# Crossing the rotary rows with small transfers in place of TensorE's sparse products, in a two-block fp32 layer stack on one core

## The chip, the cores and the metric

One NeuronCore of one Trainium2 chip runs the whole program in one launch. The metric is the device time of that launch in microseconds (us), the median of three runs. Engines are written as in the profile: PE is TensorE, DVE is VectorE, ACT is ScalarE, POOL is GpSimd, SP is SyncE, which only issues transfers. "ACTq" and "SPq" are rows of an engine's instruction sequencer (here the issuing of a transfer).

## The reference, cut to what matters

Two blocks run one behind the other on x of shape 1 x 256 x 1024 in fp32. The first is two layers of feed-forward, mixer, feed-forward. The second puts 16 meta tokens in front (L = 272 tokens) and runs two "hybrid" layers, each a sliding-window attention beside an mLSTM. The change is in the rotary step of that attention:

```python
q = rms_norm_2(aq.reshape(B, L, ATT_HEADS, ATT_HEAD_DIM), q_norm_g)
k = rms_norm_2(ak.reshape(B, L, ATT_KV_HEADS, ATT_HEAD_DIM), k_norm_g)
q = apply_partial_rope(q, cos, sin)
k = apply_partial_rope(k, cos, sin)

def apply_partial_rope(x, cos, sin):
    half = ROT_DIM // 2                       # 8
    x1, x2, rest = x[..., :half], x[..., half:ROT_DIM], x[..., ROT_DIM:]
    out = concatenate([x1 * c - x2 * s, x2 * c + x1 * s, rest])
```

Heads have 64 elements, of which the first 16 are rotated: element d (0 to 7) is mixed with element d + 8. There are 16 query heads and 2 key heads.

## The kernel before, in words

Activations lie transposed: 128 features on the partitions, tokens along the row. A 128-row chunk holds two heads. In each hybrid layer the keys are chunk c = 0 and the queries are chunks c = 1 to 8. Everything is fp32; a weight tile is split by ACT into a rounded part (`w_hi`, L1127) and by DVE into the rest (`w_lo`, L1865; every fifth unit has both in `y_both`), and PE multiplies three products for each tile (L690).

Weights come in "units" of 512 KB (up to four 128-row slabs of 256 columns) in a ring of four raw buffers, five for the split parts. The split of a unit is issued three to four units ahead of its use, between the other work of ACT and DVE, in the order of the program text. A hybrid layer streams its units in the order of `STREAM`: kv (units 0 and 1), mif (2, 3), aq (4 to 11), mqk (12 to 19), then mv, mo, ag, mg. What else is done beside unit u is in the table `VISITS`: for the rotary, `("turn", c)` at unit 5 for c = 0 and at 6 + 2 * ((c - 1) // 2) for c = 1 to 8, and `("turned", c)` at unit 5 and at 8 + 2 * ((c - 1) // 2). After it come `rt` (units 14, 15), `kx` (16) and the attention itself (`att`, from unit 18).

For one chunk, before the change:

- ACT copies the projected tile from PSUM to `k_att` or `q` (`raw_tile`, L1452), and squares it for the norm (`turn`, L1463).
- POOL multiplies it by the sine table into `qs` (L1827) and by the gained cosine table `cos_g` into `qc` (L1828). From the third chunk on it first waits for DVE's add of the chunk two before, because `qs` and `qc` have two buffers.
- PE multiplies `qs` by the 128 x 128 matrix `rot_g` (L933), which has a few +-gain entries and is otherwise zero, into PSUM.
- DVE adds that product to `qc` (`turn`, L2315) and so writes the rotated chunk back.

`tables` (L2260 to L2263) makes `cos_g` and `rot_g` on DVE once a layer. ACT's work in unit 1 of a layer is the copy of the key tile (L1452); in layer 0 the two square roots of the closing norm of the first block follow straight behind it (table load L1159, L1622, L1625), and DVE's reciprocal of L1622's result (L1887) makes `rstd`, by which every projected tile is scaled.

At the start of the program SP issues four weight loads (L540), the meta tokens (L589) and 17 small parameter loads (`parameters`, L529 and L533), and only then goes on with the weights.

## Time and profile before

| | us |
|---|---|
| median of 3 runs (lowest, highest) | 1448.73 (1448.48, 1448.89) |
| the profiled execution | 1448.88 |
| its span, first to last instruction | 1447.1 |
| PE busy | 1430.4 (99%) |
| DVE busy | 1094.8 (76%) |
| ACT busy | 854.0 (59%) |
| POOL busy | 273.1 (19%) |
| mean granted TensorE clock | 0.999 |

The chain that ended last is by engine PE 81%, DVE 11%, ACT 4%, issue 2%, DMA 1%. The transfer engines' queue of SP has 53.8% of their time, that of ACT 0.8%. The busy share is a mean over stages: PE at 99% does not say that every stage waits for PE, since a matmul's record begins when it may run and neighbours overlap; which engine is late in a stretch is read from the chain and from the idle times with their releasers. The program's stretches are: the first block up to about 915 us, hybrid layer 0 up to about 1182 us, hybrid layer 1 from there on.

### The profile page before, as it was taken

What the parts mean: (1) busy time and instruction counts of PE and PEld (TensorE: products, weight loads), DVE (VectorE), ACT (ScalarE), POOL (GpSimd) and SP (SyncE); (2) the same over time, 40 slices, a digit from 0 to 9 for tenths busy, and PEclk for the clock granted to TensorE, in tenths of its full rate; (3) what the DMA queues carried; (4) which work ended last, traced back from release to release, by engine and by line L of the source; (5) the groups of instructions that cost most, each with busy time, mean ns of one, the idle gap of its engine ahead of it and who ended that gap; (6) DMA issues with size and microseconds to landing.
All of it is one profiled execution on the core that took longest, in us unless ns stands there. A gap on an engine that the chain in (4) does not pass through costs nothing.

```text
span 1447.1 us, 27305 instructions
## 1 busy us (share of the span) xinstructions
PE 1430.4 (99%) x9633; PEld 1318.5 (91%) x9633; DVE 1094.8 (76%) x2031; ACT 854.0 (59%) x1559; POOL 273.1 (19%) x329
## 2 busy tenths in 40 slices
PE   8999999999999999999999999999999999999998
PEld 7888899988888888889988888999999999999998
DVE  6777679877756777667787766898878779976883
ACT  6665458766544666446566554656757555576762
POOL 1111113121102111014031113332250035121000
PEclk9999999999999999999999999999999999999999
DMA  6667754566565666565556565544344555434533
GB/s 211 197 194 211 233 180 131 179 185 202 183 188 182 192 187 197 185 197 164 159 171 200 181 188 175 165 143 125 89 127 142 164 154 154 127 101 123 147 119 118
DMA packets 247875, 241.25 MB, mean 167 GB/s; under 512 B 15456, under 2 KB 246736, under 8 KB 247784
## 3 DMA queue, kind: packets, MB, share of 16 engines
q1 hardware_dynamic: 244888, 236.73, 53.8%
q10 hardware_dynamic: 2896, 3.30, 0.8%
q8 instruction: 58, 0.95, 0.3%
q14 instruction: 33, 0.27, 0.1%
HBM read 238.92 MB, written 1.07 MB: 166 GB/s over the span
## 4 chain that ended last, share of the span: by engine, by line
PE 81%; DVE 11%; ACT 4%; issue 2%; DMA 1%; ACTq 0%; SPq 0%; DVEq 0%
PE bank L690 74%; DVE w_lo L1865 3%; ACT w_hi L1127 1%; DVE work L2467 1%; DVE work L2416 1%; PE bank L1010 1%; DVE work L1902 1%; PE bank L994 1%; DMA raw<-in_w_out_dram 1%; DVE y_both L1865 1%; DMA raw<-in_ffn_w_in_dram 1%; DVE work L2490 1%; PE bank L977 1%; PE bank L923 1%; ACT L1159 0%
## 5 line engine op out<-in xcount | busy, mean ns | idle before, releaser
L690 PE MATMUL bank<-x_both,w_hi 128*128 128x512 f32 (+2 forms) x3216 | 747.8, 336 | 0.9 <-DVE w_lo L1865 0.5
L1865 DVE TENSOR_TENSOR w_lo<-raw,w_hi 128x1024 fp32r<-128x1024 f32 (+1 forms) x429 | 519.4, 1234 | 203.8 <-ACT w_hi L1127 202.8
L1127 ACT CAST w_hi<-raw 128x1024 fp32r<-128x1024 f32 (+1 forms) x429 | 429.3, 1028 | 126.5 <-PE bank L690 108.2
L690 PEld LDWEIGHTS bank<-x_both,w_hi 128*128 128x128 f32 x3216 | 467.8, 189 | 3.9 <-DVE w_lo L1865 1.3
L690 PEld LDWEIGHTS bank<-x_both,w_lo 128*128 128x128 f32 x2312 | 405.8, 188 | 62.5
L690 PE MATMUL bank<-x_both,w_lo 128*128 128x256 f32 (+1 forms) x2312 | 462.2, 281 | 0.0
L690 PE MATMUL bank<-y_both,w_hi 128*128 128x512 f32 (+2 forms) x1376 | 331.5, 342 | 1.8 <-DVE w_lo L1865 1.0
L690 PEld LDWEIGHTS bank<-y_both,w_lo 128*128 128x128 f32 x1040 | 184.3, 188 | 31.3
L690 PE MATMUL bank<-y_both,w_lo 128*128 128x256 f32 (+1 forms) x1040 | 206.1, 280 | 0.0
L690 PEld LDWEIGHTS bank<-y_both,w_hi 128*128 128x128 f32 x1376 | 200.3, 189 | 2.8 <-DVE w_lo L1865 1.4
L1752 POOL TENSOR_TENSOR work<-work,rstd 128x256 f32<-128x256 f32 x88 | 67.0, 783 | 412.0 <-ACT work L1196 412.0
L1178 ACT COPY pre<-bank 128x256 f32<-128x256 f32 x176 | 56.9, 375 | 67.2 <-PE bank L690 66.9
L1208 ACT CAST y_both<-work 128x256 f32 (+1 forms) x88 | 32.7, 406 | 59.5 <-DVE work L1933 59.4
L690 PE MATMUL bank<-x_both,y_both 128*128 128x272 f32 (+1 forms) x504 | 67.6, 289 | 0.0
L1196 ACT ACTIVATE work<-work 128x256 f32<-128x256 f32 x88 | 33.2, 418 | 53.2 <-DVE work L1922 53.2
L690 PEld LDWEIGHTS bank<-x_both,y_both 128*128 128x128 f32 x504 | 63.6, 188 | 0.6
L1138 ACT ACTIVATE x_both<-h,par 128x256 fp32r<-128x256 f32 (+1 forms) x56 | 28.1, 512 | 60.6 <-DVE h L1978 52.9
L1813 POOL TENSOR_SCALAR work<-work 128x256 f32<-128x256 f32 x32 | 36.4, 1137 | 98.0 <-DVE work L2390 98.0
L1717 POOL TENSOR_TENSOR sq<-h 128x256 f32<-128x256 f32 (+1 forms) x34 | 21.4, 631 | 163.2 <-DVE h L1978 162.9
L1882 DVE SCALAR_TENSOR_TENSOR x_both<-h,par,x_both 128x256 fp32r<-128x256 f32 (+1 forms) x56 | 29.1, 528 | 25.6 <-ACT x_both L1138 25.6
L1940 DVE TENSOR_TENSOR y_both<-work,y_both 128x256 f32 (+1 forms) x88 | 33.6, 423 | 15.3 <-ACT y_both L1208 14.7
L1902 DVE TENSOR_TENSOR work<-bank,rstd 128x256 f32<-128x256 f32 (+1 forms) x98 | 37.4, 422 | 5.2 <-PE bank L690 4.9
(312 smaller groups left out, 1394.9 us busy)
## 6 DMA issues: line engine op xcount, KB each, us to landing
raw<-in_ffn_w_in_dram SPq DMA_DIRECT2D x176, 512.0 KB, 4.2
raw<-in_w_in_dram SPq DMA_DIRECT2D x100, 512.0 KB, 3.6
raw<-in_ffn_w_out_dram SPq DMA_DIRECT2D x64, 512.0 KB, 4.5
raw<-in_w_out_dram SPq DMA_DIRECT2D x32, 512.0 KB, 4.2
raw<-in_ffn_w_out_dram SPq DMA_DIRECT2D x32, 384.0 KB, 3.6
raw<-in_rec_w_in_dram SPq DMA_DIRECT2D x16, 512.0 KB, 4.0
raw<-in_sg_w_in_dram SPq DMA_DIRECT2D x16, 512.0 KB, 4.3
raw<-in_rec_w_out_dram SPq DMA_DIRECT2D x8, 512.0 KB, 3.5
```

The costliest lines, as they stand in the source:

```text
L690: i_ = mm(accs[m][:, cols], w[:, j, m * P:(m + 1) * P], moving, start=begin and g == 0 and not residual, stop=final)
L1127: nc.scalar.copy(hi_part(U)[:, 0:n, :], raw[:, s, 0:n, :]).then_inc(hi_made, 1)
L1138: i_ = activation(xview(dst, k, N), src, ACT.Copy, scale=scale)
L1178: nc.scalar.copy(ffn_b[:, m, :], bank[b][:, SEQ:2 * SEQ]).then_inc(low_copied, 1)
L1196: activation(ffn_s[:, m, :], ffn_t[:, m, :], ACT.Silu).then_inc(silu_done, 1)
L1208: nc.scalar.copy(dst, ffn_h[:, m, :]).then_inc(act_hi, 1)
L1752: TT(ffn_r[:, m, :], ffn_s[:, m, :], rstd[:, META:L], MUL).then_inc(gate_scaled, 1)
L1813: TS(pr[:, P:AW], pr[:, P:AW], rec[:, 1:2], None, MUL).then_inc(s_prob, 1)
L1865: TT(lo_part(U)[:, 0:n, :], raw[:, s, 0:n, :], hi_part(U)[:, 0:n, :].bitcast(fp32), SUB).then_inc(lo_made, 1)
L1882: i_ = STT(out=xview(dst_lo, k, N), in0=src, scalar=scale, in1=hi, op0=MUL, op1=SUB)
L1902: TT(dst, tile(pr, m, N), rstd[:, T0:L], MUL).then_inc(tile_read, 1)
L1940: TT(lo, ffn_h[:, m, :], hi.bitcast(fp32), SUB).then_inc(act_ready, 1)
```

## The change: rows crossed by transfers

- The matrix `rot`, the tile `rot_g` and PE's products are removed; PE's `turned` does nothing.
- New in ACT: `cross` issues four transfers from on-chip memory to on-chip memory. Each takes eight rows of the tile and puts them on the eight rows they are rotated with (0 to 7 with 8 to 15, and the same at 64). One call serves the key tile (8 rows x 272 each), one call each pair of query chunks (8 rows x 2 x 272, or 2 x 256 in layer 1): five calls and 20 transfers a layer. A call first waits for its copies.
- `crossed_k` is the last chunk of `qk`, `crossed_q` is `mv`; both are free at that time.
- POOL waits for the transfers and multiplies the crossed rows by `sin_g`, the sine table with its sign and the crossed gain in it. DVE makes `sin_g` where it made `rot_g`.
- DVE adds `qs` and `qc`, both from on-chip memory, and waits for POOL instead of PE.
- SP issues six more small parameter loads (the gains with their eights exchanged) in `parameters`.

```diff
-        rot_g = region(2, P)
+        sin_g = region(2)
+        crossed_k, crossed_q = qk[:, NC8 - 1, :], mv
+        crossed = [sem(f"crossed{i}") for i in range(5)]
...
+                half = ROT // 2
+                for n, src in (("attn_q_crossed", attn_q_norm_g_2), ("attn_k_crossed", attn_k_norm_g_2)):
+                    t, r, k = PAR[n]
+                    both = par_rows[r:r + k, t, :].rearrange("l (e d) -> l e d", e=2)
+                    for a, b, w in ((0, half, half), (half, 0, half), (ROT, ROT, DH - ROT)):
+                        g = src[:, b:b + w].rearrange("l (o d) -> l o d", o=1).broadcast_to((k, 2, w))
+                        sp.dma_start(both[:, :, a:a + w], g).then_inc(par_loaded, 16)
...
-                pe.wait_ge(par_loaded, 16 * 17)
+                pe.wait_ge(par_loaded, 16 * 23)
...
-                def turned(c):
...
-                    mm(bank[5 + n % 2][:, 0:L], rot_g[:, 0 if c else 1, :], qs[:, n % 2, :], start=True,
-                       stop=True).then_inc(rot_mm, 1)
...
+                def cross(i, src, dst, landed):
+
+                    half = ROT // 2
+                    act.wait_ge(tile_read, landed)
+                    for a in (0, DH):
+                        for x, y in ((a, a + half), (a + half, a)):
+                            act.dma_start(dst[x:x + half], src[y:y + half]).then_inc(crossed[i], 16)
...
                                 raw_tile(pb, 0, k_att, L)
+                                cross(4, k_att, crossed_k, 2 * pb + 1)
...
                                         raw_tile(pb + p, m, q[:, 2 * p + m, T0:L], L - T0)
+                                    cross(p, q[:, 2 * p:2 * p + 2, T0:L], crossed_q[:, 2 * p:2 * p + 2, T0:L], T + 2)
...
-                    TT(qs[:, n % 2, :], src, cst("sin"), MUL)
+                    pool.wait_ge(crossed[(c - 1) // 2 if c else 4], 64 * (l + 1))
+                    TT(qs[:, n % 2, :], crossed_q[:, c - 1, :] if c else crossed_k, sin_g[:, 0 if c else 1, :], MUL)
...
-                    TS(rot_g[:, 0, :], cst("rot"), gq, sc, MUL, MUL)
-                    TS(rot_g[:, 1, :], cst("rot"), gk, None, MUL).then_inc(cos_ready, 1)
+                    TS(sin_g[:, 0, :], cst("sin"), pcol("attn_q_crossed", l), sc, MUL, MUL)
+                    TS(sin_g[:, 1, :], cst("sin"), pcol("attn_k_crossed", l), None, MUL).then_inc(cos_ready, 1)
...
-                    dve.wait_ge(rot_mm, n + 1)
-                    TT(dst, bank[5 + n % 2][:, 0:L], qc[:, n % 2, :], ADD).then_inc(q_ready, 1)
+                    dve.wait_ge(qc_new, n + 1)
+                    TT(dst, qs[:, n % 2, :], qc[:, n % 2, :], ADD).then_inc(q_ready, 1)
```

ACT's instructions in unit 1 of layer 0, before (L1452 is the copy of the key tile, L1159 and L1622 the root and its table; names in brackets are the semaphores waited for):

```order
L1127 CAST y_both<-raw 128x1024 [waits unit_done,w_loaded0]
L1452 COPY work<-bank 128x272 [waits first_done,tile_read]
L1159 ACT_TABLE_LOAD
L1159 ACTIVATE root_of_eps<-epsc 128x1
L1622 ACTIVATE rms<-bank,eps_sq 128x272 [waits sum_done]
```

and in the changed kernel, whose line numbers differ by a few:

```order
L1122 CAST y_both<-raw 128x1024 [waits unit_done,w_loaded0]
L1447 COPY work<-bank 128x272 [waits first_done,tile_read]
L1455 DMA work<-work 8x272 [waits tile_read]
L1455 DMA work<-work 8x272 x3
L1154 ACT_TABLE_LOAD
L1154 ACTIVATE root_of_eps<-epsc 128x1
L1626 ACTIVATE rms<-bank,eps_sq 128x272 [waits sum_done]
```

Four transfers now stand between the key tile's copy and the root, with a wait for that copy. In the aq units the same four (8x544) stand between the two copies and the squares.

SP's parameter loads at the program's start, before:

```order
L529 DMA par_rows<-in_rec_gate_x_b_dram 8x128
L533 DMA par_rows<-in_attn_q_norm_g_dram 2x64 x2
L533 DMA par_rows<-in_attn_k_norm_g_dram 2x64 x2
L591 UNCONDITIONAL_BRANCH
L591 ISA
L540 ISA [waits lo_made]
L540 DMA raw<-in_ffn_w_in_dram 128x4x256
```

and in the changed kernel:

```order
L527 DMA par_rows<-in_rec_gate_x_b_dram 8x128
L531 DMA par_rows<-in_attn_q_norm_g_dram 2x64 x2
L531 DMA par_rows<-in_attn_k_norm_g_dram 2x64 x2
L538 DMA par_rows<-in_attn_q_norm_g_dram 2x2x8 x2
L538 DMA par_rows<-in_attn_q_norm_g_dram 2x2x48
L538 DMA par_rows<-in_attn_k_norm_g_dram 2x2x8 x2
L538 DMA par_rows<-in_attn_k_norm_g_dram 2x2x48
L596 UNCONDITIONAL_BRANCH
L596 ISA
L545 ISA [waits lo_made]
L545 DMA raw<-in_ffn_w_in_dram 128x4x256
```

Six loads now stand in front of the fifth weight load.

## Rows read from the trace of the kernel before

**Rows 1.** Busy time by engine in one stretch: us, busy us of each engine.

```profile
927.10:946.40 19.30, 19.30 (x158) 19.07 (x157) 18.91 (x22) 10.96 (x19) 9.73 (x8) 1.00 0.64 184
```

**Rows 2.** The chain that ended last, 915 to 1000 us: start, length, what.

```profile
939.35 1.02 PE bank L933 x4
...
946.48 1.05 ACT w_hi L1127
947.53 1.21 DVE y_both L1865
...
996.09 0.47 DVE work L2362 x2
...
996.60 0.49 PE bank L993 x2
```

**Rows 3.** Line L933, whole run: count, ns min/median/max, first and last start.

```profile
L933 PE MATMUL bank<-work x36: 392/393/497, 927.4 to 1230.5; 128*128 128x272 f32 x36
```

**Rows 4.** DVE in order of time, layer 0: start, length; brackets are idle before and releaser.

```profile
917.86 1.85 DVE L1887 RECIPROCAL rstd<-rms 128x272 f32<-128x272 f32 x1 [1.00 <-ACT rms L1622]
...
920.37 0.36 DVE L2261 TENSOR_SCALAR work<-con,par 128x272 f32<-128x272 f32 x1
920.64 0.28 DVE L2262 TENSOR_SCALAR work<-con,par 128x128 f32<-128x128 f32 x1
920.84 0.28 DVE L2263 TENSOR_SCALAR work<-con,par 128x128 f32<-128x128 f32 x1
...
927.12 2.36 DVE L1865 TENSOR_TENSOR w_lo<-raw,w_hi 128x1024 fp32r<-128x1024 f32 x2 [1.43 <-ACT w_hi L1127]
```

**Rows 5.** DVE's L1865 on `w_lo` from 915 to 975 us: ns min/median/max.

```profile
L1865 DVE TENSOR_TENSOR w_lo<-raw,w_hi x15: 1205/1220/1694, 914.5 to 974.9; 128x1024 fp32r<-128x1024 f32 x15
```

**Rows 6.** ACT in order of time, unit 1 of layer 0.

```profile
915.96 1.28 ACT L1159 ACT_TABLE_LOAD   x1
...
917.36 0.47 ACT L1622 ACTIVATE rms<-bank,eps_sq 128x272 f32<-128x272 f32 x1
```

**Rows 7.** Transfers issued by ACT, lines L1651 and L1155: ns of an issue; landing of L1155's.

```profile
L1651 ACTq DMA_DIRECT2D gate_rows<-work x2: 268/398/528, 960.1 to 1226.7; - x2
...
L1155 ACTq DMA_DIRECT2D work<-gate_rows x8: 326/326/455, 984.7 to 1372.5; - x8
...
DMA to landing us min/median/max: 3.0/3.4/4.5
```

**Rows 8.** DVE in order of time, layer 1.

```profile
1215.12 0.90 DVE L2315 TENSOR_TENSOR work<-bank,work 128x272 f32<-128x272 f32 x2 [0.38 <-PE bank L933]
...
1233.93 0.79 DVE L1902 TENSOR_TENSOR pre<-bank,rstd 128x272 f32<-128x272 f32 x2 [0.40 <-PE bank L690]
```

**Rows 9.** The program's start: SP, landing of L540's next two loads, ACT, DVE, PE.

```profile
13.16 0.55 SPq L533 DMA_DIRECT2D par_rows<-in_attn_k_norm_g_dram  x2
14.09 5.34 SPq L540 DMA_DIRECT2D raw<-in_ffn_w_in_dram  x3
...
DMA to landing us min/median/max: 4.2/4.6/4.9
...
16.58 2.94 ACT L1127 CAST w_hi<-raw 128x1024 fp32r<-128x1024 f32 x3
...
24.53 0.75 DVE L1917 TENSOR_TENSOR work<-bank,pre 128x256 f32<-128x256 f32 x2
...
25.96 0.70 PE L690 MATMUL bank<-x_both,w_hi 128*128 128x512 f32 x2
```

**Rows 10.** Chunks 1 and 2 of layer 0 on ACT and DVE; POOL's two products, whole run.

```profile
928.89 0.79 ACT L1452 COPY work<-bank 128x272 f32<-128x272 f32 x2
...
941.69 0.78 DVE L2315 TENSOR_TENSOR work<-bank,work 128x272 f32<-128x272 f32 x2
...
L1827 POOL TENSOR_TENSOR work<-work,con x18: 662/769/1631, 922.4 to 1226.0; 128x272 f32<-128x272 f32 x18
L1828 POOL TENSOR_TENSOR work<-work x18: 764/1481/1819, 923.9 to 1226.7; 128x272 f32<-128x272 f32 x18
```

More of the change, by code:

```diff
@@ L24 @@
 M_MIN = -41.0
-WORK_SLOTS = 67
+WORK_SLOTS = 69
 AW = 3 * P
@@ L36 @@
 C_AQ, C_KV, C_AG, C_MQK, C_MV, C_MIF, C_MO, C_MG = 0, 1024, 1280, 2304, 3328, 4352, 4360, 5384
-CONST_W = dict(ident=P, tri=P, amask=AW, tmask=L, mmask=P, rot=P, head_mean=2, cos=L, sin=L, k_rows=P, tail_rows=P, tail_head=ATT_H)
+CONST_W = dict(ident=P, tri=P, amask=AW, tmask=L, mmask=P, head_mean=2, cos=L, sin=L, k_rows=P, tail_rows=P, tail_head=ATT_H)
 CONST_AT = {}
@@ L61, in constants @@
     half = ROT // 2
-    for h0 in (0, DH):
-        for d in range(half):
-            c["rot"][h0 + half + d, h0 + d] = -1
-            c["rot"][h0 + d, h0 + half + d] = 1
     c["head_mean"][i, i // DH] = 1.0 / DH
@@ L77, in constants @@
             c["cos"][h0 + k:h0 + k + half] = np.cos(ang)
-            c["sin"][h0 + k:h0 + k + half] = np.sin(ang)
+            c["sin"][h0 + k:h0 + k + half] = np.sin(ang) * (1 if k else -1)
     return np.concatenate([c[n] for n in CONST_W], 1)
@@ L87 @@
     [("norm_g_2", 16), ("mlstm_conv_w_2", 64), ("mlstm_conv_b_2", 16), ("mlstm_out_norm_g_2", 16),
-     ("attn_q_norm_g_2", 2), ("attn_k_norm_g_2", 2)],
+     ("attn_q_norm_g_2", 2), ("attn_k_norm_g_2", 2), ("attn_q_crossed", 2), ("attn_k_crossed", 2)],
 ]):
@@ L443, in build_stack @@
             sem(n) for n in ("ws_tr", "ws_read", "vt_tr", "vt_read", "sg_mm", "sg_read"))
-        cos_ready, qsq_new, qc_new, turn_mm, rot_mm, q_ready = (
-            sem(n) for n in ("cos_ready", "qsq_new", "qc_new", "turn_mm", "rot_mm", "q_ready"))
+        cos_ready, qsq_new, qc_new, turn_mm, q_ready = (
+            sem(n) for n in ("cos_ready", "qsq_new", "qc_new", "turn_mm", "q_ready"))
+        crossed = [sem(f"crossed{i}") for i in range(5)]
         rs_new, rt_mm, rt_read, k_ready, tail_new = (
@@ L924, in turn @@
                     i_.then_inc(turn_mm, 1)
-                def turned(c):
-                    n = 9 * l + c
-                    pe.wait_ge(qc_new, n + 1)
-                    pe.wait_ge(cos_ready, l + 1)
-                    if c >= 2:
-                        pe.wait_ge(q_ready, n - 1)
-                    mm(bank[5 + n % 2][:, 0:L], rot_g[:, 0 if c else 1, :], qs[:, n % 2, :], start=True,
-                       stop=True).then_inc(rot_mm, 1)
                 def rt(step):
@@ L1060, in ml @@
                         i_.then_inc(m_ms, 1)
-                do = dict(turn=turn, turned=turned, rt=rt, kx=lambda n: kx(), att=att,
+                do = dict(turn=turn, turned=lambda n: None, rt=rt, kx=lambda n: kx(), att=att,
                           silu=lambda n: None, silued=lambda n: None, mvt=mvt_chunk, ml=lambda hs: ml(*hs))
```

## The prediction

> **What bounds the kernel now.** The page gives PE 99%, so one first takes every PE instruction for time on the path. I read four views to test that where the change is. First the busy time by stretch: in layer 0 from 927.1 to 946.4 us DVE is busy 18.91 of 19.30 us, as full as PE [rows 1]. Then the chain of waits: up to 946 us it runs over PE, with 1.02 us for four of the products that go, and at 946.48 us it leaves PE for ACT and DVE and comes back only at 996.60 us, when PE's L993 has waited for DVE's L2362 [rows 2]. Then DVE in order of time: it waits 1.00 us for ACT's root L1622, starts at 917.86 us, waits once more at 927.12 us (1.43 us for ACT, which itself had waited for DVE's gate row), and from there to 961 us shows no idle time [rows 4]. So in layer 0 PE and DVE run level, and the later of the two at the attention is DVE: from 917.86 to 996.6 us DVE sets the end, and each of its waits is for ACT, none for PE. Last, layer 1, where DVE is nearly as full but waits for PE: 0.38 us before the adds at 1215.12 us and 0.40 us at 1233.93 us [rows 8] (a third wait, at 1226 us, has ACT right behind it with work of its own until that time, so it gives nothing). From 1235 us on DVE sets the time there too, until the attention takes over.
>
> **What goes.** 36 PE instructions [rows 3], two for each of 18 chunks. The chain prices four at 1.02 us [rows 2], 0.255 each: 9.2 us of PE, 4.6 a layer. In layer 0 this is worth 0: PE comes to L993 4.6 us earlier and waits that much longer. In layer 1 it is worth the waits of DVE that it ends: 0.38 + 0.40 = 0.8 us; the rest is again waited off at the attention. Bounds: 0, if the adds then wait for POOL, and all 9.2 us, if I read DVE wrongly (a rival below).
>
> **What is added on ACT in unit 1 of layer 0.** Before, the table load stands at 915.96 us straight behind the key tile's copy, the root at 917.36 us straight behind the table, and DVE waits for the root [rows 6, 4]. Now a wait for the copy and four issues stand in between, and ACT's queue is empty when they come, so they cannot be covered. The nearest issues on ACT are 0.33 us (L1155) and 0.27 to 0.53 us (L1651) [rows 7]; with about 0.04 us between two, 0.37 us each, 1.5 us for four. Bounds: 4 x 0.30 = 1.2 and 4 x 0.57 = 2.3 us. All of it moves DVE's start at 917.86 us, and with it everything up to L993: +1.5 us. Behind it on ACT wait the second root, two splits and the key tile's square, and they move along with DVE.
>
> The Trainium skill says of starting transfers from several engines that it saves only the sequencer's time, "which is usually small relative to the DMA itself" (DMA: Bandwidth & Descriptors, Issuing engines are not separate DMA queues). The rows agree on the sizes, 0.3 us to issue and 3.4 us to land; by that rule one would cost the issues at nothing and come out 1.5 us lower, at +0.8. I don't, because here the small part is the one that is waited for.
>
> In layer 1 the root of the norm comes before unit 1, so the same four issues only push the two splits behind them, which DVE takes up about 1.5 us after they were ready before: 0, at most 0.6 us. The four calls in the aq units come where ACT would wait for PE's next pair anyway, and the splits behind them are made one or more us before DVE wants them: 0.
>
> **DVE's own work.** `sin_g` is 272 wide where `rot_g` was 128: by start distances 0.27 us instead of 0.20 us [rows 4], two of them, +0.14 us a layer, on DVE's path in both.
>
> **The adds.** They read `qs` from on-chip memory, where they read PSUM. DVE's split, which has both inputs on chip, takes 1.22 us alone and up to 1.69 us when POOL works beside it [rows 5]: 0.47 us for a collision. The two adds of a pair (0.78 us together [rows 10]) are the instructions beside which POOL starts its next product, three pairs a layer. The second add begins before POOL does, so it may as well win as lose: I take 0.1 us a pair, +0.3 us a layer. Bounds: -0.4 a pair (the split behind them is then spared) and +0.47.
>
> **The new wait of POOL.** For chunks 1 and 2 in layer 0: copies end at 929.7 us [rows 10] plus the 1.5 us shift, four issues to 932.7, landing 2.0 to 4.5 us later (nearest row 3.0 to 4.5 [rows 7], less for 8 rows of 2 KB): 934.7 to 937.2. Two chunks on POOL at 0.77 + 1.48 us each [rows 10] make 4.5: done 939.2 to 941.7. DVE's adds come at 941.69 + 1.5 = 943.2 us. Cover 1.5 us or more; behind the adds on DVE would stand the splits. The later pairs wait for the add of two chunks before anyway, and that comes after the landing. In layer 1 the cover is about 1 us less. I take 0, bound 0.9 us.
>
> **SP at the start.** Six loads more, at 0.55 us for two and the gap, 0.305 each [rows 9]: 1.8 us (up to 0.46 each, 2.8 us). The fifth weight load, at 14.09 us, lands after 4.2 us at 18.3 us; ACT's third split of the row at 16.58 us takes it up at 18.5 us, so 0.2 us is free and ACT, then DVE, come 1.6 us later. DVE's L1917, which frees the banks that PE's L690 at 25.96 us refills, ends at 24.95 and 25.28 us, 0.9 us before PE needs the second. So PE, which sets the time in the whole first block, loses 1.6 - 0.9 = 0.7 us; 0 to 1.7.
>
> **Sum** against the profiled execution (1448.88 us; span 1447.1 and 1.8 around it; 0.15 above the median): start +0.7; layer 0 +1.5 + 0.14 + 0.3 = +1.94; layer 1 -0.8 + 0.14 + 0.3 = -0.36. Together +2.3, so 1451.2 us for a profiled execution and 1451.0 us for the median.
>
> **The rivals.**
> - *PE is the path after all.* For it: 99% busy and the chain on PE up to 946 us and, in layer 1, to 1234 us. Against it: from 946 to 996 us the chain has no PE. It gives -9.2 + 0.7 + 1.5 = -7.0, 1441.7 us. Chance 0.08.
> - *Late landings.* A weight load of the same time takes 4.2 to 4.9 us [rows 9]; if the crossings queue behind two such and take 6 us or more, the adds of chunks 1 and 2 wait for POOL, with the splits behind them. At 6 us: in layer 0 938.7 + 4.5 = 943.2, just level, and with POOL slowed to 1.63 + 1.82 us a product pair [rows 10] 2.4 us late; in layer 1 about 3 us late. It decides from a landing of about 4.5 us, and gives +2.3 + 5 = +7, 1456 us. For it: the queue of SP is busy in these stretches. Against it: L1155's rows of a like time. Chance 0.12.
> - *The adds and POOL shut each other out.* With the collision at 0.47 us for each of 4 groups a layer, and a second one on the split behind: 8 x 2 x 0.47 = 7.5 at most, half of it likely when it happens, less my 0.6: +3, 1454 us. Chance 0.12. The Trainium skill has this as a rule: a DVE instruction with two SBUF inputs and a GpSimd instruction that reads SBUF take the shared pair of ports one at a time, for the whole instruction (SBUF — State Buffer, SBUF: two separate sides). The 1.69 us of rows 5 agree with it. It speaks against this change, since the operand moves from PSUM to SBUF.
> - *The two openings are covered.* If the fifth load lands early enough and the table load slips in before the issues, -0.7 - 1.5 leaves +0.1: 1448.8 us. Chance 0.13.
> - My forecast: 0.55.
>
> That the change fails to remove PE's work is excluded: the order of PE's instructions shows it gone.
>
> **How the numbers follow.** A measurement of this kernel tells 0.2% (2.9 us) from no change: faster is below 1445.8, slower above 1451.6. The forecast's own range, from its bounds, is 1448 to 1454: of its 0.55, 0.31 lie within 0.2% and 0.23 above, 0.01 below. The covered case adds 0.12 within and 0.01 faster; the PE case 0.08 faster; late landings and shut-out adds 0.20 slower, 0.04 within. Sum: faster 0.10, same 0.47, slower 0.43. The range leaves out the PE case and the end of the late landings: 1446.0 to 1455.5 us.
>
> **What would show it.** No L933 rows. A hole on ACT of about 1.5 us with four issues before the root in layer 0, DVE's reciprocal 1.5 us later relative to PE's sums, and a PE that waits some 4 to 6 us in total between 975 and 1000 us at L993 and its neighbours, in layer 0 and again in layer 1. PE's idle time before L690 near 26 us. DVE's adds without idle time before them. Wrong would be: PE without new idle time in layer 0 (then the time falls by much more), or DVE idle before its adds with POOL as the releaser (then it rises by more).

## The result and the profile after

| | before | changed |
|---|---|---|
| median, us (lowest to highest) | 1448.81 (1448.48 to 1448.98, 4 runs) | 1471.65 (1470.27 to 1472.35, 4 runs) |
| ratio, 95% interval | | 1.0158 (1.0146 to 1.017) |
| profiled execution, its span | 1448.88, 1447.1 | 1470.27, 1468.4 |
| PE, DVE, ACT, POOL busy | 1430.4, 1094.8, 854.0, 273.1 | 1435.0, 1096.8, 853.5, 271.0 |

The change costs 22.8 us where 2.3 were forecast, and the time lies far above the range. PE has 9.2 us less to do and is busy 4.6 us longer. Three views show how; bracketed rows and line numbers of "before" are those shown ahead of the prediction.

First the waits. This is the list of what PE waited for between 900 and 1270 us of the changed kernel (us in total, times, the longest); before had no wait for squares in it:

```profile
PE bank L928 <- ACT work L1466: 11.7, 8, 2.9
PE bank L695 <- DVE work L1908: 3.0, 1, 3.0
PE bank L988 <- DVE work L2360: 1.6, 1, 1.6
```

L928 is PE's sum of a tile's squares (L923 before), L1466 is ACT's square, L695 the weight products. All eight waits are of one kind, one for each pair of query tiles. ACT's instructions in order of time, at the key's call and at the first pair's, name the cause (start, us, engine, line; behind it the idle time and its releaser):

```profile
915.32 0.39 ACT L1447 COPY work<-bank 128x272 f32<-128x272 f32 x1 [0.21 <-PE bank L695]
915.74 3.26 ACTq L1455 DMA_DIRECT2D work<-work  x4
919.03 1.28 ACT L1154 ACT_TABLE_LOAD   x1 [3.32 <-issue]
...
920.43 0.47 ACT L1626 ACTIVATE rms<-bank,eps_sq 128x272 f32<-128x272 f32 x1
...
932.21 0.79 ACT L1447 COPY work<-bank 128x272 f32<-128x272 f32 x2
933.02 2.62 ACTq L1455 DMA_DIRECT2D work<-work  x4
935.69 0.75 ACT L1466 ACTIVATE work<-work 128x272 f32<-128x272 f32 x2 [2.70 <-issue]
936.35 1.98 ACT L1122 CAST w_hi<-raw 128x1024 fp32r<-128x1024 f32 x2
```

An issue takes 0.63 us, not 0.37: 2.62 us a call, and 3.26 for the key's, whose first takes 1.26. The key's call makes the table load start at 919.03 instead of 915.96 us [rows 6], and DVE's reciprocal at 920.94 (it waits 4.30 us for the root) instead of 917.86 [rows 4]. At the first pair the squares start 2.70 us behind the copies, with nothing between but the issues. Before, they stood directly behind the copies:

```profile
935.25 0.80 ACT L1452 COPY work<-bank 128x272 f32<-128x272 f32 x2 [2.13 <-PE bank L690]
935.95 0.75 ACT L1463 ACTIVATE work<-work 128x272 f32<-128x272 f32 x2
936.60 1.04 ACT L1127 CAST w_hi<-raw 128x1024 fp32r<-128x1024 f32 x1
```

These three rows are of the kernel before, second pair; PE took the first of these squares up at 938.28 us, 1.9 us after it was made (935.95 + 0.43); at the first pair it was 1.1 us (931.08 against 929.57 + 0.43). That is all the slack a call had: 1.1 us at the first pair of layer 0 and, worked out in the same way, 1.7 to 2.2 us at the seven other pairs.

Second, the chain of waits of the changed kernel, 930 to 966 us (start, us, what). Before, it ran over PE alone up to 946.48 us [rows 2]; now each pair repeats the same loop, copy, four issues, square, PE:

```profile
933.02 0.64 ACTq L1455
...
935.01 0.63 ACTq L1455
935.69 0.44 ACT work L1466
936.17 1.34 PE bank L928 x12
937.51 4.22 PE bank L695 x23
...
945.85 1.34 PE bank L928 x12
947.19 3.01 PE bank L695 x23
...
954.32 1.34 PE bank L928 x12
955.66 4.53 PE bank L695 x23
```

The same 23 weight products take 3.01 us once and 4.22 and 4.53 us behind two of the waits. Third, therefore, the busy time by stretch (from, to, length; busy us of PE, of PE's weight loads, of DVE, ACT and POOL; the granted clock of PE; the transfer engines' share of time and GB/s). The granted clock is the third column from the end:

```profile
937.50:942.00 4.50, 4.50 (x27) 4.50 (x27) 4.43 (x6) 1.01 (x2) 2.36 (x3) 0.65 0.61 190
947.00:955.60 8.60, 7.59 (x64) 7.37 (x63) 7.07 (x9) 3.54 (x8) 4.42 (x4) 1.00 0.48 132
955.60:960.20 4.60, 4.60 (x26) 4.60 (x26) 4.55 (x5) 0.87 (x1) 2.87 (x3) 0.63 0.41 114
1214.00:1220.00 6.00, 6.00 (x34) 6.00 (x34) 4.86 (x6) 0.75 (x2) 4.06 (x4) 0.60 0.60 176
```

The clock of PE has two levels, 1.2 and 2.4 GHz (0.5 and 1.0). Before, it stood at 1.00 in all these stretches. Now it is between them just behind several of the waits, so that a wait costs more than it lasts; "busy" grows with it. Everything from 1260 us on only stands later.

How much each kernel is late is best read at one instruction of each layer. The start of the first copy out of PSUM for the attention (DVE L2334 before) stands, against before's 973.2 and 1240.1 us, at +10.1 and +21.7 us in the changed kernel, and its span is 21.3 us longer: DVE's reciprocal of layer 1, ahead of its query tiles, is 10.3 us late (1194.7 against 1184.4). So half of the loss arises in each layer ahead of its attention (in layer 0 with the key's call in it), and nearly none elsewhere. The other kernels in the same measure:

| kernel | layer 0 | layer 1 | span |
|---|---|---|---|
| products gone, no transfers | +1.8 | +1.5 | +2.0 |
| issues alone, products kept | +12.2 | +28.6 | +28.4 |
| issues behind the squares | +2.8 | +4.2 | +3.6 |
| issues by SP | +1.0 | +2.9 | +3.7 |

How much of the loss is waiting, and how much the clock, is read beside the kernel of the first row, which has the same PE instructions. The busy time of the two, the changed kernel first:

```profile
PE 1435.0 (98%) x9597; PEld 1322.0 (90%) x9597; DVE 1096.8 (75%) x2031; ACT 853.5 (58%) x1559; POOL 271.0 (18%) x329
PE 1425.2 (98%) x9597; PEld 1313.5 (91%) x9597; DVE 1096.7 (76%) x2031; ACT 853.6 (59%) x1559; POOL 275.2 (19%) x329
```

The spans are 1468.4 and 1449.1 us, 19.3 apart. PE is busy 9.8 us longer with the same work, and idle 33.4 us instead of 23.9, 9.5 more. The granted clock gives nearly the same for the first part: it is 0.89 from 930 to 975 us and 0.85 from 1195 to 1230 us, where the other kernel has 1.00, and 45 x 0.11 + 35 x 0.15 = 10.2 us. The second part is less than the 14.7 us of new waits (11.7 and 3.0), since PE then waits less ahead of and in the attention (3.8 us from 900 to 1290 us, the other kernel 10.1). So what the transfers cost is about half waiting and half clock.

### The profile page after: what moved, and what is told of

It reads as the page before. It is cut to its first block, busy times and chain, and to the rows that moved or that the text cites. A ratio compares the mean times of both kernels' runs of the same rounds, so it can differ in the third digit from the quotient of the medians.

```text
span 1468.4 us, 27263 instructions
## 1 busy us (share of the span) xinstructions
PE 1435.0 (98%) x9597; PEld 1322.0 (90%) x9597; DVE 1096.8 (75%) x2031; ACT 853.5 (58%) x1559; POOL 271.0 (18%) x329
## 4 chain that ended last, share of the span: by engine, by line
PE 77%; DVE 12%; ACT 5%; issue 3%; ACTq 2%; SPq 1%; DMA 1%; DVEq 0%
PE bank L695 71%; DVE w_lo L1871 3%; ACTq L1455 2%; ACT w_hi L1122 1%; DVE work L2473 1%; DVE work L2422 1%; PE bank L1005 1%; DVE work L1908 1%; PE bank L928 1%; PE bank L989 1%; DVE y_both L1871 1%; DVE work L2496 1%; PE bank L972 1%; ACT L1154 0%; ACT y_both L1122 0%
## 5 line engine op out<-in xcount | busy, mean ns | idle before, releaser
L695 PE MATMUL bank<-x_both,w_hi 128*128 128x512 f32 (+2 forms) x3216 | 752.9, 339 | 2.2 <-DVE w_lo L1871 1.7
L1122 ACT CAST w_hi<-raw 128x1024 fp32r<-128x1024 f32 (+1 forms) x429 | 429.0, 1028 | 122.1 <-PE bank L695 103.6
L695 PEld LDWEIGHTS bank<-x_both,w_hi 128*128 128x128 f32 x3216 | 473.5, 192 | 5.2 <-DVE w_lo L1871 2.7
L695 PE MATMUL bank<-x_both,w_lo 128*128 128x256 f32 (+1 forms) x2312 | 465.4, 282 | 0.0
L695 PEld LDWEIGHTS bank<-x_both,w_lo 128*128 128x128 f32 x2312 | 409.0, 190 | 62.4
L695 PE MATMUL bank<-y_both,w_hi 128*128 128x512 f32 (+2 forms) x1376 | 331.5, 342 | 1.8 <-DVE w_lo L1871 1.1
L695 PEld LDWEIGHTS bank<-y_both,w_lo 128*128 128x128 f32 x1040 | 184.3, 188 | 31.3
L695 PE MATMUL bank<-y_both,w_lo 128*128 128x256 f32 (+1 forms) x1040 | 206.1, 280 | 0.0
L695 PEld LDWEIGHTS bank<-y_both,w_hi 128*128 128x128 f32 x1376 | 200.3, 189 | 2.7 <-DVE w_lo L1871 1.3
L695 PE MATMUL bank<-x_both,y_both 128*128 128x272 f32 (+1 forms) x504 | 68.8, 292 | 3.0 <-DVE work L1908 3.0
L695 PEld LDWEIGHTS bank<-x_both,y_both 128*128 128x128 f32 x504 | 64.6, 192 | 3.6 <-DVE work L1908 3.2
L1871 DVE TENSOR_TENSOR y_both<-raw,y_both 128x1024 fp32r<-128x1024 f32 x27 | 33.6, 1243 | 10.8 <-ACT y_both L1122 10.8
```

The lines of the kernel that those rows point to most:

```text
L695: i_ = mm(accs[m][:, cols], w[:, j, m * P:(m + 1) * P], moving, start=begin and g == 0 and not residual, stop=final)
L1122: nc.scalar.copy(hi_part(U)[:, 0:n, :], raw[:, s, 0:n, :]).then_inc(hi_made, 1)
L1871: TT(lo_part(U)[:, 0:n, :], raw[:, s, 0:n, :], hi_part(U)[:, 0:n, :].bitcast(fp32), SUB).then_inc(lo_made, 1)
```

## The experiments

The theory at the outset, A: ACT's 0.63-us issues stand in its order ahead of the squares that PE waits for, and this is nearly all of the loss. B: part of it is the clock behind the waits. The rivals: the landing of the transfers with POOL's and the adds' port; SP's loads at the start; and, on the gain side, that PE's freed 9.2 us would have shown if nothing else had been in the way.

### Taking the issues away

`e1_products_gone`. The change without its transfers:

```diff
-                                cross(4, k_att, crossed_k, 2 * pb + 1)
...
-                                    cross(p, q[...], crossed_q[...], T + 2)
...
-                    pool.wait_ge(crossed[(c - 1) // 2 if c else 4], 64 * (l + 1))
-                    TT(qs[:, n % 2, :], crossed_q[:, c - 1, :] if c else crossed_k, sin_g[...], MUL)
+                    TT(qs[:, n % 2, :], src, sin_g[...], MUL)
```

> The changed kernel without the 40 crossing transfers and without GpSimd's waits for them; GpSimd multiplies the uncrossed rows, so the crossing itself is left out. Everything else of the change stays (no products on TensorE, the adds from SBUF, the six small loads). Theory A (ACT's issues ahead of the squares and splits are the whole cost): 1447 to 1449 us, no wait of PE for the squares, granted clock 1.00 from 915 to 1265 us. If PE's products had been on the path (36 x about 0.4 us of which 9 us in waits or work): about 1440. If port contention of adds and GpSimd or the start loads are the cost: 1455 or more.

Measured: 1450.97 us (1449.29 to 1454.34, 11 runs), ratio 1.0018 (1.0009 to 1.0027). So 20.7 us go with the transfers and 2.3 stay. That is 2 us above what A said, so the transfers are nearly all and not all of it, and it is nowhere near the 1440 of a gain from PE. Its waits of PE, same view as above, tell what became of the 9.2 us:

```profile
PE bank L988 <- DVE work L2357: 4.0, 2, 2.0
PE bank L985 <- issue: 2.4, 2, 1.3
PE bank L988 <- DVE work L2365: 1.9, 4, 0.6
PE bank L942 <- DVE work L2302: 1.8, 2, 1.3
```

10 us, all at `rt` (L942) and the attention's first steps and behind DVE or nothing: PE comes earlier and waits there.

### The issues alone

`e2_issues_alone`. The kernel before, plus:

```diff
+                                cross(4, cst("sin"), crossed_k, 2 * pb + 1)
...
+                                    cross(p, con[:, ...], crossed_q[...], T + 2)
...
+                    if c == NC8:
+                        for i in range(5):
+                            pool.wait_ge(crossed[i], 64 * (l + 1))
```

> The kernel before, its rotation by TensorE unchanged, with the 40 transfers issued by ACT at the places of the change but from rows of constants into rows that nobody reads; GpSimd waits for all of a layer only at its last turn. Theory A: these issues alone cost what the change costs or more, 1468 to 1475 us, with PE waits for the squares of 1 to 3 us a pair and a granted clock of 0.6 to 0.8 behind them. Rival (landings, GpSimd's waits and the adds' port are the cost): within 3 us of before, 1449 to 1452.

Measured: 1477.15 us (1474.2 to 1478.3, 4 runs), ratio 1.0193 (1.0178 to 1.0209). That is 2 us above what A said. With no reader of the transfers, no new add and no start load, the loss is there in full: this ends the rival of landings and ports. It is even 5.5 us slower than the changed kernel, which also has the other 2.3 us: where the issues hold PE up, PE sets the time, and then its missing products are worth about 8 of their 9.2 us (5.5 + 2.3, a sum that takes the 2.3 us over from `e1_products_gone`). Its chain of waits runs through the products in the pairs' loop, 1.02 us at 947.37 us and 2.02 at 957.00. In `e1_products_gone`, where DVE sets it, they were worth nothing.

### The same issues, behind what is waited for

`e3_behind_squares`, the changed kernel with its calls moved (it has lost them at their old places, which the lines below leave out):

```diff
+                            if u == 1:
+                                cross(4, k_att, crossed_k, 2 * pb + 1)     # behind the two roots
...
                             for kind, n in [... the squares of the pair ...]:
                                 do[kind](n)
+                            if j == 1 and ph == "aq":
+                                cross(p, q[...], crossed_q[...], T + 2)
```

> The changed kernel with ACT's issues moved behind what PE and DVE wait for: the key's four behind the two roots of layer 0, each query pair's four behind the pair's squares. Same count of transfers and the same computation. Theory A: PE's waits for squares shrink to under 0.5 us, the clock stays at 1.00 and the time is 1450 to 1457 (the splits still stand behind 2.6 us of issues). Rival that any 2.6 us of ACT costs the same wherever it stands: 1466 to 1472. Rival of late landings: slower than 1471, since they land 1 to 3 us later.

Measured: 1452.69 us (1451.98 to 1454.61, 6 runs), ratio 1.0033 (1.0021 to 1.0045). The same 40 issues at 0.64 us, in other places, cost 1.7 us instead of 20.7. ACT's order of time at the first pair (as above):

```profile
931.50 0.79 ACT L1447 COPY work<-bank 128x272 f32<-128x272 f32 x2
932.18 0.43 ACT L1466 ACTIVATE work<-work 128x272 f32<-128x272 f32 x1
932.32 0.63 ACTq L1455 DMA_DIRECT2D work<-work  x1
932.51 0.42 ACT L1466 ACTIVATE work<-work 128x272 f32<-128x272 f32 x1
932.99 1.96 ACTq L1455 DMA_DIRECT2D work<-work  x3
935.04 2.00 ACT L1122 CAST w_hi<-raw 128x1024 fp32r<-128x1024 f32 x2 [2.11 <-issue]
```

The splits L1122 now start 2.11 us late, and the time hardly moves: DVE has room for late splits, PE had none for late squares.

### The start loads

`e4_no_start_loads`, on the changed kernel:

```diff
-                for n, src in (("attn_q_crossed", attn_q_norm_g_2), ("attn_k_crossed", attn_k_norm_g_2)):
-                    ... (six dma_start)
...
-                    TS(sin_g[:, 0, :], cst("sin"), pcol("attn_q_crossed", l), sc, MUL, MUL)
+                    TS(sin_g[:, 0, :], cst("sin"), gq, sc, MUL, MUL)
```

> The changed kernel without its six small parameter loads at the start; the sine tables take the uncrossed gains, which leaves out the exchange of the gains. My sum gave these loads 0.7 us: 0.7 us faster than the changed kernel, about 1471. If they cost nothing: 1471.6; all else as the changed kernel, with PE waits for squares and the clock drops.

Measured: 1469.0 us (1468.06 to 1469.47, 4 runs), 2.65 us below the changed kernel, which was measured at another time, with nearly the same time of before (1448.6 against 1448.8). At the marks used above it stands 0.6 us ahead of the changed kernel in layer 0 and 2.0 in layer 1. In its trace, 0.6 us arise up to layer 0 and 1.4 behind it, where nothing was changed; they stay open (the changed kernel's own runs spread over 2.1 us). In `e1_products_gone` the chain of waits of the first 27 us runs over SP's issues, which it didn't before:

```profile
15.28 0.26 SPq L538
15.58 0.26 SPq L538
15.88 0.27 SPq L538
...
16.53 3.75 DMA raw<-in_ffn_w_in_dram
...
26.66 103.36 PE bank L695 x591
```

One issue every 0.30 us, and PE's L695 at 26.66 us against 25.96 [rows 9]: 0.7 us, the forecast's figure, by the path it named. But one execution doesn't show the size. In the changed kernel's own the same PE instruction stood at 25.73 us, since SP came to the weight load 0.9 us earlier, with the same six loads in front. Over all the kernels, the long run of PE that starts there begins between 25.5 and 27.4 us in the ten that have the six loads and between 25.4 and 27.3 us in the six that don't, with means of 26.6 and 26.5. The chain of waits runs over SP in seven of the ten (in one it doesn't reach back so far) and in none of the six. So the path is real in some executions, and no cost of the loads stands out of the scatter.

### What the clock takes

`e5_pe_kept_busy`, on the changed kernel, and later `e13_key_behind_kept_busy`, the same edit on `e11_key_behind_root` (below):

```diff
+KEPT = (10, 4, 4, 4)
...
+                    if c % 2:
+                        keep_warm(6, KEPT[(c - 1) // 2])
                     pe.wait_ge(qsq_new, n + 1)
```

> The changed kernel with small spare products put on TensorE ahead of its wait for each query pair's first squares (10 for the first pair of a layer, 4 for the others, about 0.25 us each): the waits stay as long as they were, but TensorE isn't idle in them. Theory B (about half of the loss is the granted clock that falls after these waits): granted clock 0.97 or more in 930 to 975 and 1195 to 1230 us, and 1457 to 1463 us. Rival that the waits alone make the loss and the clock is a side effect of little worth: 1470 to 1473.

> The kernel with only the key's issues moved (1470.4 us, where TensorE's waits for squares are the one thing left that the trace names: 12.8 us over 8 waits, with a granted clock of 0.85 in 930 to 975 and 1195 to 1230 us), with the spare products of the earlier experiment ahead of the pairs' first squares. If the clock behind these waits made the rest of the 17.7 us that the pairs' issues cost: clock 1.00 in both stretches and 1460 to 1464 us. If the clock is worth little: over 1467.

Measured: 1465.87 us (1463.07 to 1468.24, 4 runs) against 1471.65, and 1464.59 (1460.53 to 1466.16, 4 runs) against 1470.44. Both kernels are 5.8 us faster with the spare products, above the first's expected 1457 to 1463 and just above the second's 1460 to 1464. The stretches of the first show that only part of the clock came back: before 930 us the key's wait, which the spare products don't cover, took it down, to the lower level from 925 to 930. Layer 0 gained next to nothing (its mark is at 984.1 us against 983.3, with a start 1.1 us later), and 4.3 us were gained between the two marks.

```profile
915.00:930.00 15.00, 11.97 (x71) 11.47 (x69) 10.02 (x17) 7.51 (x11) 4.18 (x4) 0.80 0.38 111
930.00:975.00 45.00, 44.65 (x365) 43.81 (x365) 35.94 (x55) 23.88 (x40) 17.48 (x17) 0.99 0.50 146
1195.00:1230.00 35.00, 33.79 (x277) 33.41 (x276) 27.34 (x36) 14.94 (x24) 12.48 (x11) 0.95 0.53 152
```

(The changed kernel: 0.89 from 930 to 975 and 0.85 from 1195 to 1230 us.) In the sum used above, 15 x 0.20 + 45 x 0.01 + 35 x 0.05 = 5.2 us were still missing, of 10.2. The second's clocks are 0.92 and 0.95, not the 1.00 expected: 5.4 us missing, of 12.0 in the kernel without spare products (0.85 in both stretches). So 5.8 us were had where 5 to 7 us of clock came back. That is a lower bound of the clock's share and agrees with B's half of the loss; that the rest would come back too is not shown.

### What an issue's price hangs on

`e6_issues_from_dram`, `e2_issues_alone` with the source of each transfer in DRAM:

```diff
-                                cross(4, cst("sin"), crossed_k, 2 * pb + 1)
+                                cross(4, consts[:, ...], crossed_k, 2 * pb + 1)
```

> The kernel before with the 40 issues by ACT in the same places, of the same shapes and into the same rows, but read from DRAM (rows of the constants) rather than from on-chip rows; nobody reads what they bring. If the 0.63 us of an issue belongs to the on-chip source: issues of 0.27 to 0.37 us, half the waits, 1455 to 1463 us. If it belongs to the shape (8 partitions, or this engine in this stage): 0.63 us and 1474 to 1478 us, as with the on-chip source.

Measured: 1451.8 us (1450.67 to 1452.47, 10 runs), ratio 1.0021 (1.0012 to 1.0031): 25 us less than with the on-chip source, and below the expected 1455 to 1463. The issues of the two kernels (minimum, median, maximum in ns, first and last start):

```profile
L1462 ACTq DMA_DIRECT2D work<-con x40: 631/643/1258, 917.4 to 1246.9; - x40
```

```profile
L1462 ACTq DMA_DIRECT2D work<-in_consts_dram x40: 278/317/557, 916.1 to 1223.5; - x40
```

A call is then 1.3 us, inside the slack but for the first pair of layer 0, and PE's waits for squares shrink to 0.5 us. The transfers' shapes and places are alike; the source alone doubles the price.

### The adds on GpSimd

`e7_pool_adds`, on `e3_behind_squares`:

```diff
                     TT(qc[:, n % 2, :], src, cos_g[...], MUL).then_inc(qc_new, 1)
+                    pool.wait_ge(qc_new, n + 1)
+                    pool.wait_ge(qsq_new, n + 1)
+                    TT(src, qs[:, n % 2, :], qc[:, n % 2, :], ADD).then_inc(q_ready, 1)
...
                 def turn(c):      # DVE
-                    TT(dst, qs[:, n % 2, :], qc[:, n % 2, :], ADD).then_inc(q_ready, 1)
+                    return
...
+                    dve.wait_ge(q_ready, 9 * (l + 1))
```

> The kernel with the issues behind the squares (1452.7 us), and the 18 additions made by GpSimd behind its two products instead of by DVE. DVE loses 9 x 0.43 = 3.9 us of work a layer in a stage that it sets. If DVE's own work is what counts: 1446 to 1449 us, faster than before. Rival: GpSimd's additional 9 x 1 us a layer slows DVE's splits beside it (1.14 us alone, 1.72 beside GpSimd) by as much as is saved: 1451 to 1455.

Measured: 1454.86 us (1453.82 to 1455.71, 5 runs), 2.2 us slower than with the adds on DVE. DVE's groups from 915 to 996 us, first of the kernel with the adds on DVE, then of this (busy us, mean ns):

```profile
L1873 DVE TENSOR_TENSOR w_lo<-raw,w_hi 128x1024 fp32r<-128x1024 f32 x18 | 22.9, 1288 | 2.6 <-ACT w_hi L1122 2.5
L2424 DVE SCALAR_TENSOR_TENSOR work<-pre,par,work 128x272 f32<-128x272 f32 x18 | 8.5, 500 | 1.7 <-ACT work L1662 1.5
L2323 DVE TENSOR_TENSOR work<-work 128x272 f32<-128x272 f32 x9 | 3.6, 433 | 0.0
```

```profile
L1876 DVE TENSOR_TENSOR w_lo<-raw,w_hi 128x1024 fp32r<-128x1024 f32 x17 | 22.7, 1353 | 2.6 <-ACT w_hi L1122 2.5
L2427 DVE SCALAR_TENSOR_TENSOR work<-pre,par,work 128x272 f32<-128x272 f32 x18 | 9.5, 559 | 1.7 <-ACT work L1662 1.5
```

In this stretch DVE loses 3.6 us of adds and gets back 65 ns a split (1.2 us) and 59 ns a tap (1.0 us). Over the whole run it is busy 1098.9 us, against 1096.7 with the 18 adds in it: what it was relieved of came back, and more, in longer instructions, of which only these two groups were looked at one by one. The rival held. At the marks used above the kernel stands 0.7 us behind in layer 0 and 2.9 in layer 1; what makes layer 1 the worse isn't shown.

### SP issues, and the gains crossed on chip

`e8_sp_issues`, the changed kernel with this in SP's program in place of ACT's calls:

```diff
+                        if ul == KEY_AT:                     # 8
+                            cross(4, l, k_att, crossed_k, ...)
+                        if ul in PAIRS_AT:                   # 13, 15, 17, 19
+                            cross(c // 2, l, q[...], crossed_q[...], ...)
                         load(U, ...)
```

> The changed kernel with the 40 transfers issued by SP between its weight loads (the key's ahead of the stream's load 8, the pairs' ahead of loads 13, 15, 17 and 19), so ACT issues none and nothing of its order moves; all else as changed, the same computation. Theory A: ACT's place in the order was the cost, so about the time of the kernel with no transfers at all (1451.0): 1450 to 1453 us, no wait of PE for squares. Rival (SP's loads come late behind 2.6 us of issues, or the transfers' landing holds GpSimd and then DVE): 1455 to 1465, with waits of ACT's splits for the weight loads or of DVE for GpSimd.

Measured: 1452.45 us (1451.35 to 1453.57, 7 runs), ratio 1.0028 (1.0017 to 1.004). ACT's program is as before's and PE waits for no square. On SP the issues take 0.65 us as well, and the kernel stands 1.5 us above `e1_products_gone`, which has no transfers.

`e9_sp_and_gains`: that, with the six start loads replaced:

```diff
-                        sp.dma_start(both[:, :, a:a + w], g).then_inc(par_loaded, 16)
...
+                    small.append((gain_x[x:x + n, :], par[y:y + n, t, r:r + 2 * DEPTH]))
```

> The kernel with SP issuing the transfers (1452.5 us), and the six small gain loads at the start replaced by six on-chip transfers of the gain columns among the small loads of the first output phase; the same computation as the changed kernel. If the start loads cost what the order of SP's queue says (0.7 us) or what the medians of the changed kernel with and without them say (2.6 us): 1450.0 to 1451.8 us. If they cost nothing: 1452.4. It is below before's 1448.5 only if the freed TensorE time counts, which theory E (DVE sets the end of these stages) denies.

Measured: 1451.63 us (1449.46 to 1453.1, 11 runs), ratio 1.0019 (1.001 to 1.0028). 0.8 us less, the size of the 0.7 us of SP's queue, but the ranges overlap and a gain isn't shown; 3.1 us above before.

### How the loss depends on length and place

`e10_two_of_four`, on the changed kernel:

```diff
-                    for a in (0, DH):
+                    for a in (0,):
...
-                    pool.wait_ge(crossed[...], 64 * (l + 1))
+                    pool.wait_ge(crossed[...], 32 * (l + 1))
```

`e11_key_behind_root`, the key's call alone moved:

```diff
                                 raw_tile(pb, 0, k_att, L)
-                                cross(4, k_att, crossed_k, 2 * pb + 1)
...
+                            if u == 1:
+                                cross(4, k_att, crossed_k, 2 * pb + 1)
```

> The changed kernel with two issues a call instead of four (rows of the first head of each tile alone are crossed, the second's are left out), in the same place of ACT's order. 20 issues fewer, 1.26 us less ahead of each call's squares. Theory A as a wait with slack (PE's squares have about 1.9 us to spare a call, so 1.3 us are nearly hidden but for the first pair and the root): 1454 to 1458 us. Rival that each issue costs its 0.5 us wherever it stands (20.7 us over 40 issues): 1461 us.

> The changed kernel with the key's four issues moved behind the two roots of layer 0 alone; the query pairs' issues stay ahead of the squares. Theory A by places: the late root costs 3.0 us (PE's one wait for DVE at the fourth unit), so 1466.5 to 1469 us, and the rest of the loss stays with the pairs. If the key's call makes most of the loss: under 1462.

Measured: 1453.31 us (1452.75 to 1453.76, 6 runs), and 1470.44 (1469.25 to 1471.17, 4 runs). Half of the issues cost 2.3 us beside `e1_products_gone`, all of them 20.7: a wait with slack, not a price per issue (and 0.7 us under the least that A said). PE's waits for squares fall to 1.5 us. The key's call, whose 3.0-us wait of PE goes, is worth 1.2 us only. That is 1.4 us above what A said: the pairs' waits grow in its place, from 11.7 to 12.8 us in sum.

### The freed time of TensorE

`e12_products_kept`, on `e1_products_gone`, and `e14_sp_gains_products`, on `e9_sp_and_gains`:

```diff
+                def turned(c):
+
+                    pe.wait_ge(qc_new, n + 1)
+                    mm(bank[5 + n % 2][:, 0:L], ident, qs[:, n % 2, :], start=True, stop=True).then_inc(rot_mm, 1)
...
+                        pool.wait_ge(rot_mm, n - 1)
```

> The kernel without transfers (1451.0 us; the crossing left out, adds from SBUF, sine tables and start loads kept), with 18 products of 128x272 put back on TensorE where the rotation's stood; nobody reads them, GpSimd alone waits for them before it overwrites their input. If DVE sets these stages and the removal is worth nothing: 1450.5 to 1451.8 us, as without them. If TensorE's freed time was worth what it holds (9 us over both layers) and something else of the change ate it: 1455 or more.

> The kernel with SP's transfers and the gains exchanged on chip (1451.6 us), with 18 products of 128x272 put back on TensorE that nobody reads; the computation is the reference's. In the pair of kernels without transfers the same products made it 0.6 us faster (1451.0 to 1450.4), with the clock at 1.00 in 1230 to 1260 us instead of 0.94. If it is so that TensorE's freed time turns into waits and a lower clock: 1450.0 to 1451.3 us. If that pair was chance, or the products hold GpSimd's turns up: 1451.6 to 1453.

Measured: 1450.39 us (1449.4 to 1450.79, 11 runs) against 1450.97 without, and 1450.76 (1450.07 to 1454.47, 11 runs) against 1451.63. The products put back cost nothing; both pairs are 0.6 and 0.9 us faster with them. The intervals overlap, so a gain isn't shown; that their removal is worth nothing is. The stretches 1240 to 1250 and 1250 to 1255 us, first without them, then with:

```profile
1240.00:1250.00 10.00, 6.96 (x51) 6.43 (x50) 9.33 (x26) 4.66 (x10) 0.00 (x0) 1.00 0.37 105
1250.00:1255.00 5.00, 5.00 (x30) 4.98 (x29) 4.24 (x16) 4.42 (x10) 1.25 (x2) 0.66 0.46 129
```

```profile
1240.00:1250.00 10.00, 10.00 (x78) 9.81 (x77) 9.37 (x26) 4.67 (x9) 0.00 (x0) 1.00 0.38 105
1250.00:1255.00 5.00, 5.00 (x41) 4.93 (x40) 4.49 (x20) 4.50 (x11) 1.56 (x2) 1.00 0.48 139
```

DVE is busy 9.33 and 9.37 of 10 us in both. PE, rid of its products, is idle 3 us of them, and then gets a clock of 0.66.

## Why the prediction was wrong

**The step that failed** is "The four calls in the aq units come where ACT would wait for PE's next pair anyway, and the splits behind them are made one or more us before DVE wants them: 0." Those 0 us were 20.7, less the key's share (1.2 us, below). Two things were wrong in it. I looked only at the splits behind the calls, and not at the two squares that stand between, which PE reads with 1.7 to 2.2 us to spare (1.1 at the first pair of layer 0). And an issue took 0.63 us, outside the bounds of 0.30 to 0.57 from [rows 7]: none of those rows had source and target on chip. At the forecast's 0.37 us, 1.5 us a call would have stayed within the slack but at the first pair of layer 0; `e6_issues_from_dram`, where an issue is 0.32 us, is the nearest to the forecast's case on the chip, at 1451.8 us.

**The account of the 22.8 us**: 2.3 stay without the transfers. Of the other 20.5, about half is PE's waiting: 14.7 us of new waits (11.7 for squares, 3.0 for the bank behind the late root), less what it no longer waits for around the attention, 9.5 us in sum. The other half is the clock behind the waits: 9.8 us more of busy time for the same work, of which the runs with spare products show 5.8. Neither was one of my rivals: each of these took the new wait to be POOL's or DVE's, and none the clock.

**The root in unit 1 of layer 0**, +1.5 us: right in place, +3.1 in size at DVE's reciprocal (0.82 us an issue with the long first one). Its worth in the end was 1.2 us (`e11_key_behind_root`), because the pairs' waits behind it took up the rest.

**What goes.** "In layer 0 this is worth 0" and, in layer 1, 0.8: right in the kernels in which DVE sets the time (`e1_products_gone` against `e12_products_kept`: +0.6, so 0 within the error, where 0.8 was forecast). In the changed kernel it is worth about 8 us (the sum under `e2_issues_alone`), since there PE is the one that is late. The waits at L993 and its neighbours, forecast as 4 to 6 us a layer, came as 10 us together in `e1_products_gone`.

**The adds and tables**, +0.44 us a layer: DVE's copy for the attention is 1.8 - 0.7 = 1.1 us late in layer 0 of `e1_products_gone`. The adds take 432 ns, as from PSUM (430), and have no idle time before them; the splits are 28 ns longer each (1292 to 1320, 18 of them) and their kin that write `y_both` 24 (five), 0.6 us together. Which instruction is the longer one differs: in `e3_behind_squares`, with the same adds, the splits take 1288 and 1219 ns, but its L2041 (L2033 before) 926 instead of 709. Over the whole run DVE is busy 1096.7 us in each of `e1_products_gone`, `e3_behind_squares` and `e8_sp_issues`, 1.9 us more than before, of which the tables are 0.3. So the rival in which both shut each other out fell with the adds as made, and came true when POOL got more to do (`e7_pool_adds`).

**POOL's new wait**, 0: right. It waited 11.65 us for the landing of the first pair, 4.0 us after the last issue, and nobody waited for it. With the same landings in `e3_behind_squares` and `e8_sp_issues` the loss is gone, so late landings are ruled out as the cause.

**SP at the start**, +0.7: the path named is seen in seven of the ten traces with the loads; the size isn't shown. It is 0.7 us in one trace and 0.8 between `e8_sp_issues` and `e9_sp_and_gains`, whose ranges overlap, and over all traces PE's start scatters by 2 us with and without the loads.

**The rule of the Trainium skill** that issuing is "usually small relative to the DMA itself" (DMA: Bandwidth & Descriptors, Issuing engines are not separate DMA queues) was weighed for the root alone. The changed kernel's trace agrees with its comparison (0.63 us to issue, 4.0 to land), and by it the four calls cost nothing, as I had it. The measurement decides otherwise: POOL was done with the first two chunks 4.9 us before DVE's add wanted them (943.4 and 948.3 us), so the landing was covered, and the issues had only 1.1 to 2.2 us.

Open: the 1.4 us behind the start by which the kernel without start loads was faster; how much of the clock's other 4 us or so could be had back; and the 0.4 us in layer 0 of `e1_products_gone` that neither its late start, tables nor splits name (1.8 - 0.7 - 0.14 - 0.6). No version tried was faster than the kernel before. The best complete one, `e14_sp_gains_products`, stands at a ratio of 1.0015 (1.0006 to 1.0024), 1.9 us above the 1448.9 of before measured beside it.

## What to carry to other kernels

An issue is an instruction of the engine that makes it. Before putting transfers into an engine's order, list each instruction behind them with its reader and the time between the two, and compare the shortest of these with the whole block of issues: under it they are free (1.3 us a call here), over it they set the pace (2.6 us). A move of work away from TensorE pays only where the time is TensorE's: here the same products were worth 0 us in one kernel and about 8 in another. And a wait of TensorE can cost more than it lasts: read the granted clock behind it. If small transfers are the way, let SP issue them, or put them behind the last instruction that another engine is waiting for.

## What was not expected of the hardware

- The issue of a transfer of 8 partitions takes 0.63 us on ACT and 0.65 on SP when its source and its target are on chip, and 0.32 us when its source is in DRAM. The first of a series can take 1.26 us. Whether it reads one tile of a row or two (8.5 and 16 or 17 KB) makes no difference.
- In the changed kernel, PE waits of 1.0 to 2.9 us were followed by stretches at a granted clock of 0.57 to 0.68 (0.80 once), but those of 0.70 us before 945.85 us and 0.83 us before 1242.85 us were not, nor was in that execution the one of 3.0 us before 923.32 us, where the same wait in `e5_pe_kept_busy` had 0.50 behind it. With spare products in the waits the clock was 0.99 from 930 to 975 us in that kernel and 0.92 in `e13_key_behind_kept_busy`.
